# Moving every buffer that TensorE reads to a 512-byte boundary in a two-block sequence-model kernel

## The chip, the cores and the metric

The kernel runs on one core of a Trainium2 chip. The metric is the device time of one launch in microseconds (us); less is better. The program is one straight line of instructions for each engine, tied together by semaphores.

## What is computed

The reference is a small network on 256 tokens of 1024 features, batch 1: two mixer blocks with residuals (a state-space mixer, then latent attention), a norm, and a third block with sparse attention beside a gated convolution, a feed-forward part and a gated embedding. Cut to its shape:

```
h = x
u = rms_norm(h);  h = h + ssd_mixer(u) @ ssm_out_w        # projections 1024 -> 2048+4096+32, 2048 -> 1024
u = rms_norm(h);  h = h + mla_mixer(u) @ mla_out_w        # 1024 -> 384+256+64+2048, 16 heads, 2048 -> 1024
h = rms_norm(h)
h = h + (sparse attention and gated convolution of rmsnorm(h), merged by sigmoid gates) @ w_out_2
h = h + ffn(rmsnorm(h)) @ w_down_2                         # 1024 -> 2 x 2816 -> 1024
h = h + ple_gate(rmsnorm(h)) * (p @ w_ple_2)
out = rmsnorm(h)
```

Nearly all of the arithmetic is in the projections: matrices of weights, in float32, each read once, against 256 tokens.

## The kernel before

**Layout.** Activations lie feature-major: 128 features on the partitions, 256 tokens (1,024 B) along the row. A projection's output tile of 128 features is the sum over its k tiles of `weights[128 x 128].T @ activations[128 x 256]`.

**Precision.** A float32 value is split into a high part in the type float32r and the rest, also float32r. TensorE makes three matmuls for each pair of tiles (lines 628 to 630): weights high by activations high, weights high by activations low, weights low by activations high. In the profile's rows these are `ps<-uh,wh`, `ps<-ul,wh` and `ps<-uh,wl`: what is written, then the moving operand (256 columns of activations, 1,024 B of each partition), then the stationary operand (128 columns of weights, 512 B of each partition). Each matmul has a weight load of its own, a PEld row. In two places the roles are swapped: "V" jobs and "C" jobs (lines 635 to 637, `ps<-wh,uh` and the like) hold activations still and move weights.

**Weights.** They come in 254 slabs of 8 blocks (4,096 B of each partition) through a ring of 6 buffers `raw` (SP issues the loads), ScalarE makes `wh` (line 1122), GpSimd makes `wl` (line 571), both with rings of 6. One slab is 8 blocks, and so 24 matmuls. The order of the jobs is written out by hand in `weight_jobs`, and no scheduler moves anything.

**Memory.** Each `sb(...)` takes the next free bytes of a partition, in the order of the lines, after 16,384 B of DMA scratch and four small constants, so the first one starts at 16,512. Behind them lies an arena of 105 KiB, in which `ar(...)` places the buffers of a phase one behind the other, rounded up to 32 B: `uh`, `ul` (the normed input of every block), then by phase `ynh`, `ynl`, `ogh`, `ogl`, `cqh`, `cql`, `ckh`, `ckl`, `cnh`, `cnl`, `onh`, `onl`, `mh`, `ml`, `cxh`, `cxl`, `ffh`, `ffl`, `ph`, `pl`. A buffer's start is therefore whatever the sizes ahead of it leave. A row of `uh` is 1,024 B and a block of `wh` 512 B, so all rows and blocks of a buffer have the start's remainder by 512.

Of the kernel before, what the change touches and what calls it, by code (L numbers as in the profile page):

```python
# [18 lines left out]
P = 128  # L19
T = 256  # L20
TB = T // P
DM = 1024
KD = DM // P
# [33 lines left out]
FIRST_SLABS = 2  # L57
FIRST_COLS = 8
WARM_UP = 20


def weight_jobs():
# [186 lines left out]
def vector_columns():  # L249

    at, c = {}, 0
    for name, n in [("norm0", 8), ("norm1", 8), ("final1", 8), ("sconv_w", SSM_CT * SSM_TAPS), ("sconv_b", SSM_CT),
                    ("ssm_d", 16), ("ssm_nw", 16), ("dt_bias", 1), ("a_log", 1), ("qnorm", 3), ("kvnorm", 2),
                    ("g_mix", 8), ("pos_k", 16), ("pos_v", 16), ("conv_w", CONV_CT * CONV_TAPS), ("conv_b", 4),
                    ("ln_g", 4), ("ln_b", 4), ("b_co", 8), ("g_ffn", 8), ("fconv_w", 2 * KF * FF_TAPS),
                    ("fconv_b", 2 * KF), ("g_ple", 8), ("g_final", 8)]:
        at[name] = c
        c += n
    return at, c
# [7 lines left out]
def build(nc, slabs_dram, vec_dram, const_dram, x_dram, p_dram, out_dram):  # L267
# [4 lines left out]
    VC, n_vec = vector_columns()  # L272
    ctx = ExitStack()
    with ctx:
        def sb(name, shape, dt=f32):
            return ctx.enter_context(nc.sbuf_tensor(name, shape, dt))


        raw = sb("raw", [P, RAW_RING, SLAB])
        wh = sb("wh", [P, PART_RING, SLAB], f32r)  # L280
        wl = sb("wl", [P, PART_RING, SLAB], f32r)
        h = sb("h", [P, KD, T])
        sq = sb("sq", [P, KD, T])
        vec = sb("vec", [P, n_vec])
        cst = sb("cst", [P, N_CONST])
        ident_b = sb("ident_b", [P, P], bf16)
        mask_s = sb("mask_s", [P, P], bf16)
        cmp_add = sb("cmp_add", [P, P], bf16)
        ones = sb("ones", [P, P])
        sqsum = sb("sqsum", [P, 2, T])  # L290

        msq, root, step = sb("msq", [P, 2 * TB]), sb("root", [P, 2 * TB]), sb("step", [P, 2 * TB])
        late = sb("late", [P, T])
        late_tok = sb("late_tok", [P, TB])
        root1 = sb("root1", [P, TB])
        gain12 = sb("gain12", [P, KD])
        ident = cst[:, 0:128]
        swap = cst[:, 128:256]
        cmp_ok = cst[:, 896:1024]
# [9 lines left out]
        cursor = [0]  # L309
# [3 lines left out]

        def ar(name, shape, dt=f32):
            n = int(np.prod(shape)) * 4
            t = nc.alloc_sbuf_tensor_at(name, [P] + list(shape), dt, offset=base + cursor[0])
            cursor[0] += -(-n // 32) * 32
            assert cursor[0] <= arena_kb * 1024, (name, cursor[0])
            return t


        HEADS = 4
        phase()
        uh, ul = ar("uh", [KD, T], f32r), ar("ul", [KD, T], f32r)
        after_u = cursor[0]
        ynh, ynl = ar("ynh", [16, T], f32r), ar("ynl", [16, T], f32r)
        xs, bT, cT = ar("xs", [16, T]), ar("bT", [8, T]), ar("cT", [8, T])
        acp = ar("acp", [3 * P], f32r)
        sel = ar("sel", [SSM_H], f32r)
# [119 lines left out]
        def sem(name):  # L449
            if name not in sems:  # L450
                sems[name] = ctx.enter_context(nc.semaphore(name))
            return sems[name]
# [140 lines left out]
        def _(pe):  # L593
# [103 lines left out]
            pe.wait_ge(sem("memset"), 2)  # L697
            for _ in range(WARM_UP):
                nc.tensor.matmul(PS_TR[:, 0:P], ones[:], ones[:], start=True, stop=True)
# [1643 lines left out]
```

## Time and profile before

| | |
|---|---|
| median of 3 runs | 867.47 us (866.96 to 868.33) |
| profiled execution, first to last instruction | 865.4 us |
| TensorE (PE) busy, matmul records | 847.8 us, 98% of the span, 7,055 records |
| weight loads (PEld) busy | 816.2 us |
| GpSimd / VectorE / ScalarE busy | 624.1 / 526.8 / 485.7 us |
| DMA queues | 51.9% of 16 engines' span on the weights' queue |
| mean granted TensorE clock | 0.994 of full speed |

How to read it: matmul records overlap, since each one lasts some 280 ns in the trace while the next starts some 118 ns after it. Busy time and the mean duration of a matmul therefore don't tell the engine's pace. Its pace is the distance from one start to the next, which a timeline gives in full and a table by windows gives as length over count (about two matmuls more are counted than start inside a window, because records reach over its edges).

### The profile page before, as it was taken

To read this page: it belongs to the slowest core of one execution; us is meant where nothing else is said; L and a number is where in the kernel's file an instruction comes from. 1 tells how busy PE (TensorE), PEld (TensorE's weight loads), DVE (VectorE), ACT (ScalarE), POOL (GpSimd) and SP (SyncE) were. 2 spreads that over 40 slices of the span, in tenths; PEclk is the share of its full clock that TensorE was granted. 3 is DMA by queue.
4 is the path that set the end of the run, shared out by engine and by line. 5 is a ranking of instruction groups with operands and counts; after the bars stand their busy time and mean duration, and the time that the engine had idled before them with its cause. 6 is when DMAs were issued, how large, how long until landed. Compare 5 with 4: busy or idle time off the path is not lost.

```text
span 865.4 us, 18278 instructions
## 1 busy us (share of the span) xinstructions
PE 847.8 (98%) x7055; PEld 816.2 (94%) x7055; DVE 526.8 (61%) x1543; ACT 485.7 (56%) x925; POOL 624.1 (72%) x282
## 2 busy tenths in 40 slices
PE   8999999999999999999999999999999999999995
PEld 8999988889998899999999999988999999999995
DVE  5997758883243535445458998875566676641164
ACT  6755476664446456563846457875644544554361
POOL 4899756655997455563979899455868888889680
PEclk9999999999999999999999999999999999999997
DMA  8666633332774343433566577433646666667511
GB/s 331 192 219 218 193 99 98 99 98 75 220 218 155 114 145 107 140 99 122 162 204 190 180 210 222 127 95 116 184 144 204 177 192 182 187 193 221 170 49 50
DMA packets 38678, 138.46 MB, mean 160 GB/s; under 512 B 4416, under 2 KB 4544, under 8 KB 38592
## 3 DMA queue, kind: packets, MB, share of 16 engines
q1 hardware_dynamic: 38592, 137.30, 51.9%
q8 instruction: 56, 0.92, 0.5%
q14 instruction: 30, 0.25, 0.1%
HBM read 136.23 MB, written 1.05 MB: 159 GB/s over the span
## 4 chain that ended last, share of the span: by engine, by line
PE 80%; DVE 4%; issue 2%; ACT 1%; POOLq 0%; POOL 0%; ACTq 0%; DVEq 0%
PE ps L628 22%; PE ps L629 22%; PE ps L630 21%; DVE ps L1720 1%; PE ps L850 1%; PE ps L756 1%; PE ps L673 1%; PE ps L655 1%; PE ps L637 1%; PE ps L635 1%; PE ps L636 1%; PE ps L874 1%; PE ps L983 1%; PE ps L846 1%; PE ps L821 1%
## 5 line engine op out<-in xcount | busy, mean ns | idle before, releaser
L571 POOL TENSOR_TENSOR wl<-raw,wh 128x1024 fp32r<-128x1024 f32 x254 | 606.9, 2413 | 199.1 <-ACT wh L1122 198.9
L628 PE MATMUL ps<-uh,wh 128*128 128x256 f32 (+1 forms) x1248 | 352.4, 282 | 1.9 <-POOL wl L571 0.8
L629 PE MATMUL ps<-ul,wh 128*128 128x256 f32 (+1 forms) x1248 | 348.7, 279 | 0.0
L630 PE MATMUL ps<-uh,wl 128*128 128x256 f32 (+1 forms) x1248 | 348.3, 279 | 0.0
L1122 ACT ACTIVATE wh<-raw 128x1024 fp32r<-128x1024 f32 (+1 forms) x255 | 262.9, 1052 | 85.8 <-PE ps L630 77.9
L628 PEld LDWEIGHTS ps<-uh,wh 128*128 128x128 f32 (+1 forms) x1248 | 233.8, 187 | 3.7 <-issue 1.6
L629 PEld LDWEIGHTS ps<-ul,wh 128*128 128x128 f32 (+1 forms) x1248 | 233.7, 187 | 0.0
L630 PEld LDWEIGHTS ps<-uh,wl 128*128 128x128 f32 (+1 forms) x1248 | 233.2, 187 | 0.1
L1813 DVE TENSOR_TENSOR h<-ps,h 128x256 f32<-128x256 f32 x32 | 13.6, 425 | 103.8 <-PE ps L630 103.7
L629 PE MATMUL ps<-ffl,wh 128*128 128x256 f32 x176 | 49.3, 280 | 0.0
L628 PE MATMUL ps<-ffh,wh 128*128 128x256 f32 x176 | 49.1, 279 | 0.0
L630 PE MATMUL ps<-ffh,wl 128*128 128x256 f32 x176 | 49.1, 279 | 0.0
L1720 DVE SCALAR_TENSOR_TENSOR ps<-cpad,vec,ps 128x256 f32<-128x256 f32 x120 | 48.6, 480 | 0.0
L1611 DVE TENSOR_TENSOR fraw<-ps,late 128x256 f32<-128x256 f32 x44 | 18.4, 421 | 38.7 <-PE ps L630 38.6
L1720 DVE SCALAR_TENSOR_TENSOR ps<-sraw,vec,ps 128x256 f32<-128x256 f32 x96 | 38.9, 478 | 0.0
L1720 DVE SCALAR_TENSOR_TENSOR ps<-fraw,vec,ps 128x256 f32<-128x256 f32 x88 | 38.1, 481 | 0.0
L628 PE MATMUL ps<-ynh,wh 128*128 128x256 f32 x128 | 36.1, 282 | 0.0
L628 PE MATMUL ps<-ogh,wh 128*128 128x256 f32 x128 | 36.1, 282 | 0.0
L630 PE MATMUL ps<-ynh,wl 128*128 128x256 f32 x128 | 35.8, 280 | 0.0
L629 PE MATMUL ps<-ynl,wh 128*128 128x256 f32 x128 | 35.7, 279 | 0.0
L630 PE MATMUL ps<-ogh,wl 128*128 128x256 f32 x128 | 35.7, 279 | 0.0
L629 PE MATMUL ps<-ogl,wh 128*128 128x256 f32 x128 | 35.6, 278 | 0.0
(363 smaller groups left out, 1690.8 us busy)
## 6 DMA issues: line engine op xcount, KB each, us to landing
raw<-slabs SPq DMA_DIRECT2D x255, 512.0 KB, 4.0
h<-x_fm SPq DMA_DIRECT2D x4, 256.0 KB, 4.1
out_fm<-outb SPq DMA_DIRECT2D x4, 256.0 KB, 2.2
cst<-shape_consts SPq DMA_DIRECT2D x1, 768.0 KB, 8.4
vec<-vectors SPq DMA_DIRECT2D x1, 299.5 KB, 8.6
pin<-p_fm SPq DMA_DIRECT2D x1, 256.0 KB, 3.8
raw<-slabs SPq DMA_DIRECT2D x1, 128.0 KB, 2.8
vec<-vectors SPq DMA_DIRECT2D x1, 4.0 KB, 2.4
```

The source lines that it names most:

```text
L571: nc.gpsimd.tensor_tensor(wl[:, s % PART_RING, :], raw[:, s % RAW_RING, :], wh[:, s % PART_RING, :].bitcast(f32), ALU.subtract).then_inc(s ...
L628: nc.tensor.matmul(res, w_h, a_h, start=first, stop=False)
L629: nc.tensor.matmul(res, w_h, a_l, start=False, stop=False)
L630: ins = nc.tensor.matmul(res, w_l, a_h, start=False, stop=last)
L635: nc.tensor.matmul(res, a_h, w_h, start=first, stop=False)
L636: nc.tensor.matmul(res, a_h, w_l, start=False, stop=False)
L637: ins = nc.tensor.matmul(res, a_l, w_h, start=False, stop=last)
L655: ins = nc.tensor.matmul(PS_M[:, n.col + c:n.col + c + 1], src[:, b * P:(b + 1) * P], ones[:, 0:1], start=n.summed or k == g * per, stop=n ...
L1122: nc.scalar.activation(wh[:, s % PART_RING, 0:n], raw[:, s % RAW_RING, 0:n], ACT.Copy)\
L1611: tt(dst, o[0:rows, 0:T], late[0:rows, :], ALU.mult).then_inc(sem("dve_evac"), 1)
L1720: return stt(dst, src, w, dst, ALU.mult, ALU.add)
L1813: tt(h[:, k, :], o[:, 0:T], h[:, k, :], ALU.add).then_inc(sem("dve_evac"), 1)
```

## The change

No instruction is added, removed or moved on any engine: the five engines' lists are the same row for row but for the source's line numbers. The memory map changes alone.

- A helper `start_at` puts a gap before the next `sb` buffer, so that it begins at a multiple of 512. It stands ahead of `raw`, `wh`, `wl`, ahead of `h`, and ahead of `ones`.
- `vec` and the small columns (`msq`, `root`, `step`, `late_tok`, `root1`, `gain12`) are allocated first, ahead of the slabs.
- `ar` rounds the start of each buffer of 512 B or more up to a multiple of 512, and of 256 to 511 B up to a multiple of 256.

```diff
+PIECE = 512
+STATIONARY_AT = 0
...
+        def start_at(offset):
+
+            gap = (offset - nc.sbuf_base) % PIECE
+            if gap:
+                sb(f"gap{nc.sbuf_base}", [P, gap // 4])
+
+        vec = sb("vec", [P, n_vec])
+        msq, root, step = sb("msq", [P, 2 * TB]), sb("root", [P, 2 * TB]), sb("step", [P, 2 * TB])
+        late_tok = sb("late_tok", [P, TB])
+        root1 = sb("root1", [P, TB])
+        gain12 = sb("gain12", [P, KD])
+        start_at(STATIONARY_AT)
         raw = sb("raw", [P, RAW_RING, SLAB])
         wh = sb("wh", [P, PART_RING, SLAB], f32r)
         wl = sb("wl", [P, PART_RING, SLAB], f32r)
+        start_at(0)
         h = sb("h", [P, KD, T])
         sq = sb("sq", [P, KD, T])
-        vec = sb("vec", [P, n_vec])
...
+        start_at(0)
         ones = sb("ones", [P, P])
...
         def ar(name, shape, dt=f32):
             n = int(np.prod(shape)) * 4
+            if n >= PIECE // 2:
+                cursor[0] += -cursor[0] % (PIECE if n >= PIECE else PIECE // 2)
             t = nc.alloc_sbuf_tensor_at(name, [P] + list(shape), dt, offset=base + cursor[0])
```

What comes out of it, as the start's remainder by 512 and, in brackets, by 128:

```
buffers                                              before       after
raw, wh, wl, h, sq                                   128 (0)      0
uh, ul, ynh, ynl, ogh, ogl, cqh, cql, ckh, ckl,
ffh, ffl, xs, vn, bT, cT, qr, kr, kn, qn             448 (64)     0
cnh, cnl, gm                                         96 (96)      0
mh, ml, onh, onl, cxh, cxl, ph, pl, npn, npT         480 (96)     0
pn, pT                                               64 (64)      0
ones, sqsum                                          256 (0)      0
cst, ident_b                                         0            0
```

A remainder of 64 by 128 is still a multiple of 64; one of 96 is a multiple of 32 only.

## Rows read from the trace of the kernel before

**Rows 1.** The page, parts 1 and 2: busy TensorE and its granted clock

```profile
PE 847.8 (98%) x7055; PEld 816.2 (94%) x7055; DVE 526.8 (61%) x1543; ACT 485.7 (56%) x925; POOL 624.1 (72%) x282
...
PEclk9999999999999999999999999999999999999997
```

**Rows 2.** Waits of TensorE: total us, times, longest

```profile
PE ps L673 <- DVE root L1572: 2.5, 1, 2.5
PE ps L1089 <- ACT sq L1135: 1.9, 1, 1.9
```

**Rows 3.** Groups of matmuls by form: count, busy us, mean ns

```profile
L628 PE MATMUL ps<-uh,wh 128*128 128x256 f32 x1240 | 350.0, 282 | 1.9 <-POOL wl L571 0.8 <-DVE wl L1657 0.5 <-DVE gm L1611 0.3
...
L629 PE MATMUL ps<-ffl,wh 128*128 128x256 f32 x176 | 49.3, 280 | 0.0
...
L628 PE MATMUL ps<-ynh,wh 128*128 128x256 f32 x128 | 36.1, 282 | 0.0
L628 PE MATMUL ps<-ogh,wh 128*128 128x256 f32 x128 | 36.1, 282 | 0.0
...
L628 PE MATMUL ps<-cqh,wh 128*128 128x256 f32 x72 | 21.2, 295 | 0.0
...
L628 PE MATMUL ps<-mh,wh 128*128 128x256 f32 x64 | 18.1, 282 | 0.0
...
L628 PE MATMUL ps<-onh,wh 128*128 128x256 f32 x32 | 9.2, 288 | 0.0
...
L628 PE MATMUL ps<-ph,wh 128*128 128x256 f32 x16 | 4.6, 289 | 0.0
```

**Rows 4.** Windows: us, busy (and count) of PE, PEld, DVE, ACT, POOL; clock, DMA

```profile
645.00:820.00 175.00, 175.00 (x1488) 175.00 (x1487) 91.56 (x239) 85.29 (x121) 148.07 (x62) 1.00 0.64 189
...
604.00:636.00 32.00, 32.00 (x269) 32.00 (x269) 17.92 (x49) 19.38 (x34) 26.31 (x11) 1.00 0.59 186
```

**Rows 5.** Windows over eight stretches with a denser rhythm, and their sum

```profile
141.60:144.10 2.50, 2.50 (x23) 2.50 (x24) 2.25 (x10) 1.57 (x4) 1.13 (x1) 1.00 0.70 188
...
399.50:415.60 16.10, 16.10 (x140) 15.99 (x140) 9.55 (x18) 6.24 (x14) 5.02 (x4) 1.00 0.24 67
...
sum 46.10, PE 46.10 PEld 45.99 DVE 32.33 ACT 25.96 POOL 30.35; mean PE 5.76 PEld 5.75 DVE 4.04 ACT 3.24 POOL 3.79
```

**Rows 6.** Timeline of TensorE, 402 to 416.5 us: start us, duration, instruction

```profile
402.12 0.28 PE L628 MATMUL ps<-ogh,wh 128*128 128x256 f32 x1
...
415.49 0.28 PE L629 MATMUL ps<-ogl,wh 128*128 128x256 f32 x1
415.60 0.28 PE L630 MATMUL ps<-ogh,wl 128*128 128x256 f32 x1
415.72 0.32 PE L628 MATMUL ps<-ogh,wh 128*128 128x256 f32 x1
415.87 0.28 PE L629 MATMUL ps<-ogl,wh 128*128 128x256 f32 x1
```

**Rows 7.** Timeline where the roles are swapped: weights move, activations stand

```profile
489.11 0.28 PE L635 MATMUL ps<-wh,uh 128*128 128x256 f32 x1
...
494.10 0.28 PE L637 MATMUL ps<-wh,ul 128*128 128x256 f32 x1
...
500.12 0.29 PE L637 MATMUL ps<-wh,cxl 128*128 128x256 f32 x1
...
501.90 0.28 PE L637 MATMUL ps<-wh,cxl 128*128 128x256 f32 x1
```

**Rows 8.** Timeline of the float32r matmuls that move 64 columns

```profile
525.15 0.28 PE L629 MATMUL ps<-hgl,wh 128*128 128x64 f32 x1
...
526.26 0.28 PE L630 MATMUL ps<-hgh,wl 128*128 128x64 f32 x1
```

**Rows 9.** The page, part 5: what GpSimd and ScalarE do for each slab

```profile
L571 POOL TENSOR_TENSOR wl<-raw,wh 128x1024 fp32r<-128x1024 f32 x254 | 606.9, 2413 | 199.1 <-ACT wh L1122 198.9
...
L1122 ACT ACTIVATE wh<-raw 128x1024 fp32r<-128x1024 f32 (+1 forms) x255 | 262.9, 1052 | 85.8 <-PE ps L630 77.9
```

More of the change, by code:

```diff
@@ L288, in build @@
         cmp_add = sb("cmp_add", [P, P], bf16)
+        start_at(0)
         ones = sb("ones", [P, P])
         sqsum = sb("sqsum", [P, 2, T])
-        msq, root, step = sb("msq", [P, 2 * TB]), sb("root", [P, 2 * TB]), sb("step", [P, 2 * TB])
         late = sb("late", [P, T])
-        late_tok = sb("late_tok", [P, TB])
-        root1 = sb("root1", [P, TB])
-        gain12 = sb("gain12", [P, KD])
         ident = cst[:, 0:128]
```

## The prediction

> **What bounds the kernel now.** I read the page first: TensorE is busy 98% of the span, and its clock is granted in full in all slices but the last [rows 1]. The waits agree: the longest of TensorE's own is 2.5 us, the next 1.9 us [rows 2]. So the time is TensorE's pace, and nothing else is worth reading until that pace is known. The groups by form give the counts, three matmuls for each row shown [rows 3]. Those with a moving operand at remainder 448 are `uh` 1,240, `ff` 176, `yn` 128, `og` 128, `cq` 72 and a group `ck` of 32: 3 x 1,776 = 5,328 matmuls. Those with an operand that is a multiple of 32 only are `mh` 64, `on` 32, `ph` 16, and `cn` and `cx`, 32 each: 3 x 176 = 528. With 48 `wh,uh` that makes 5,904, all 256 columns wide. The mean durations there, 279 to 295 ns, say nothing of the pace.
>
> The pace is in the windows. From 645 to 820 us, the feed-forward part, 1,488 records lie in 175 us, two of them from over the edge: 175 / 1,486 = 117.8 ns from start to start [rows 4]. From 604 to 636 us, where `mh` and `ml` and `onh` move, it is 32 / 267 = 119.9 ns [rows 4]. 256 columns at the granted level of 2.4 GHz are 106.7 ns, so 11 ns of each matmul are not columns. At 117.8 ns the 5,904 matmuls are 695 us of 865: one nanosecond of pace is worth 5.9 us.
>
> **Does the pace depend on addresses?** Three readings.
>
> First, the same buffers run at two paces. From 402.12 to 415.49 us there are 118 steps on `ogh`, `ogl` (remainder 448): 13.37 / 118 = 113.3 ns [rows 6]. Then one matmul comes late (415.72 to 415.87, 150 ns instead of 113), and the same buffers go on at 117.8 ns. There are eight such dense stretches, 46.1 us in all [rows 5], about 400 matmuls. The DMA share is 0.70 in one of them and 0.24 in another, 0.64 in the stretch at 117.8 ns [rows 4, 5], so it isn't traffic. It reads like a rhythm between the two reads that TensorE makes at once, the moving rows and the next weights: a rhythm that a disturbance can set to either of two modes, and which then stays.
>
> Second, the swapped jobs. With the weights moving (remainder 128, a multiple of 128) and `uh` standing (448), the last 44 steps of the job take 4.99 us, 113.4 ns [rows 7]. With `cxh`, `cxl` standing (480, a multiple of 32 only) 15 steps take 1.78 us, 118.7 ns [rows 7]. Same line, same shape, same moving buffer: only the stationary address differs.
>
> Third, the multiples of 32: 119.9 against 117.8 ns, as above. So operands that are off a 64-byte boundary cost 2 to 5 ns, and a moving operand on a multiple of 128 was always in the dense mode in the one job that has both on multiples of 64.
>
> **The parts of the change.** (a) 5,328 matmuls: moving operand from 448 to 0, weights from 128 to 0. (b) 528 matmuls: from a multiple of 32 to 0. (c) the 48 swapped ones: 128 and 448 to 0 and 0. (d) `vec` and the small columns move ahead of the slabs, `ones`, `sqsum`, `pn` and the like are realigned: no instruction is added, so the cost is nothing unless an access gets slower; VectorE and ScalarE have 39% and 44% of the span free [rows 1]. If that cover were gone, a whole slab's work would show: GpSimd takes 2.41 us and ScalarE 1.05 us for each slab [rows 9], and TensorE takes 24 x 117.8 = 2.83 us.
>
> The trace has no matmul with both operands on 0, so the new pace is bounded by rows. Below: the 64-column float32r matmuls make 10 steps in 1.11 us, 111 ns, though they have a quarter of the columns [rows 8]; that is what a weight load of its own leaves, and a step can't be much shorter. Above: 119.9 ns, the worst steady pace seen [rows 4]. I take 113.3 ns, the dense mode, because the change puts the moving operand where it stood in rows 7 and because it is a mode that these very buffers already reach.
>
> The sum, against the profiled execution (865.4 us):
> - (a) about 350 of the 5,328 are in the dense mode already, and some 80 have a wait in their step. 4,900 x (117.8 - 113.3) = 22.0 us.
> - (b) some 500 without a wait, 500 x (119.9 - 113.3) = 3.3 us.
> - (c) and (d): nothing.
> - Given back: TensorE waits little now, and would wait for GpSimd only below 2.41 / 24 = 100.5 ns a step, so nothing is taken off. A slab would take 2.72 us.
>
> Together 25.3 us, so 840.1 us in the profile. The profiled span is 2.1 us under the median of the runs, and 867.5 - 25.3 = 842.2; **I forecast 842 us**.
>
> **A page that says otherwise.** The Trainium skill, page "TensorE: Matmul & The Clock Gate", section "Step-by-step: what each phase is for", says that TensorE has two independent read ports into SBUF and that loading the next tile's weights takes no bandwidth from the running matmul; its section "Back-to-back issue gap" gives columns / 2.4 + 2.5 ns, an estimate of 109.2 ns here. By that every matmul here would run at 109.2 ns before and after, and the change would do nothing. The trace differs, 117.8, 113.3 and 119.9 ns at one shape, so I keep the rows. The rule that addresses don't matter is the second rival below, worked out from rows there.
>
> **The rivals.**
>
> *More than the dense mode (0.22).* If the extra time is an access more because a row straddles a boundary, the aligned read loses it altogether and the weight load is left, 111 ns [rows 8]. Then (a) is 4,900 x 6.8 = 33.3 us, the 350 dense ones give 350 x 2.3 = 0.8, and (b) 500 x 8.9 = 4.5: 38.6 us, so 829 us. For it: off-boundary operands cost time already. Against it: in no place does a 256-column matmul go below 113.
>
> *The addresses don't decide the mode (0.22).* The two modes stand at the same addresses in rows 6, so alignment to 64 may be all that addresses do, and the mode is set by chance. Then (a) stays at 117.8, and (b) falls to it: 500 x 2.1 = 1.1 us, 866.4 us, 0.13% and no change that can be measured. For it: `ogh` in both modes. Against it: the swapped job, dense in 44 steps on end. If not even the multiples of 32 gain, it is 867.5 us. This is the case that the skill's page on TensorE stands for.
>
> *The two reads meet (0.18), the case on the other side.* Now the moving rows and the weights start at different remainders (448 and 128, or 128 and 448). Afterwards both start at 0. If the two reads collide when they want the same slice of the memory at once, equal starts are the worst case, and every matmul takes at least the pace of the worst stretch: 5,328 x 2.1 = 11.2 us, the 350 dense ones lose 350 x 4.5 = 1.6 more, (c) 0.3: +13 us, 880.5 us. It decides from a mean of 118.1 ns on, 0.3 ns x 5,904 = 1.8 us or 0.2%. For it: the two modes look like two phases of just such a meeting. Against it: they have met in some way in all stretches, since a sweep over 1,024 B beside one over 512 B passes every remainder, and 118 is what that gives.
>
> **How the numbers follow.** The forecast has 0.38. A change of under 0.2%, 1.7 us, can't be told from none in a measurement of this kernel. Faster is the forecast and the first rival, with a mixture of modes that gives part of the 25 us counted to the forecast: 0.38 + 0.22 = 0.60. Same is 0.21, since a sliver of the second rival would fall above 0.2%; slower is 0.19. The range goes from 827 us, just below the 111 ns case, to 872 us, past the no-change case and into the small end of the collision: it leaves out most of the 0.18 of that rival. The likeliest case's own range is 836 to 852 us: 836 if the pace is 112.3 ns, 852 if only 60% of (a) goes into the dense mode.
>
> **What would show it.** In the changed kernel's trace the window over the feed-forward part should hold 175 us / 113.3 ns = 1,545 starts for each 175 us instead of 1,486, and `mh`, `ml` the same pace as `uh`, `ul`, with no stretch at 117.8. The waits of TensorE should stay under some 3 us each, and GpSimd's idle time should shrink by about as much as the span. If the windows still show 1,486, the second rival holds; if `mh` alone moves, it holds exactly. If the pace is above 118.1 ns everywhere, the starts at an equal remainder are to blame. My forecast would also be wrong if the pace falls but GpSimd or a DMA becomes what TensorE waits for, which the waits would name.

## The result and the profile after

The changed kernel takes 878.98 us (median of 4 runs, 878.83 to 879.70), the kernel before 867.82 us on the same chip (866.96 to 868.33). The ratio is 1.013, with a 95% interval of 1.0116 to 1.0145: **the change made the kernel slower by 11.2 us**, where 25 us of gain were forecast. That is under 2%, but far outside what the runs of either kernel differ by. The profiled execution spans 877.2 us, 11.8 us more than that of before.

The page's line of busy time and its line of TensorE's clock answer to [rows 1], its two group lines to [rows 9]:

```profile
PE 860.2 (98%) x7055; PEld 829.0 (95%) x7055; DVE 529.8 (60%) x1543; ACT 485.7 (55%) x925; POOL 623.4 (71%) x282
...
PEclk9999999999999999999999999999999999999998
...
L583 POOL TENSOR_TENSOR wl<-raw,wh 128x1024 fp32r<-128x1024 f32 x254 | 606.1, 2412 | 211.4 <-ACT wh L1134 211.1
...
L1134 ACT ACTIVATE wh<-raw 128x1024 fp32r<-128x1024 f32 (+1 forms) x255 | 262.7, 1051 | 89.3 <-PE ps L642 85.5
```

The picture is the same one, stretched: TensorE busy for 98% at a full clock, the other engines with the same work, and more idle time before GpSimd's slabs (211.4 us instead of 199.1), because the ring comes free later. ScalarE's and GpSimd's groups have the same durations. VectorE is busy for 3.0 us more (529.8 instead of 526.8), in a few single operations; the largest change is one addition to `h` near the end, the longest of eight in this row, 2.68 us where the longest before was 1.85. No wait of TensorE grew by it:

```profile
L2233 DVE TENSOR_TENSOR h<-h,pt x8: 424/504/2682, 842.9 to 865.4; 128x256 f32<-128x256 f32 x8
```

TensorE's waits answer to [rows 2] and haven't moved:

```profile
PE ps L685 <- DVE root L1584: 2.5, 1, 2.5
PE ps L1101 <- ACT sq L1147: 1.9, 1, 1.9
```

So again only the pace is left. The first window of [rows 4], then a window inside the same `ogh`, `ogl` matmuls that were dense in [rows 6]; they stand later in the trace than before, since the kernel is slower. Columns as there. Under it are the same two matmuls of the swapped job as in [rows 7]:

```profile
645.00:820.00 175.00, 175.00 (x1462) 175.00 (x1461) 95.95 (x261) 84.93 (x120) 145.78 (x62) 1.00 0.60 184
...
408.00:420.00 12.00, 12.00 (x102) 12.00 (x101) 7.21 (x12) 4.13 (x10) 1.53 (x1) 1.00 0.13 42
```

```profile
495.94 0.28 PE L647 MATMUL ps<-wh,uh 128*128 128x256 f32 x1
...
501.22 0.28 PE L649 MATMUL ps<-wh,ul 128*128 128x256 f32 x1
```

175 us over 1,460 matmuls are 119.9 ns a step, where before it was 117.8. The dense `ogh`, `ogl` stretch of [rows 6] has gone as well: 12 us over 100 matmuls are 120.0 ns, where it was 113.3. So has that of the swapped job: 44 steps in 5.28 us are 120.0 ns, where it was 113.4. There is nearly one pace now and no other. Counted start by start over the whole trace, leaving out each step over 126 ns (those hold a wait):

```
float32r matmuls of 256 columns     before     after
steps                                5,789     5,790
mean                              117.6 ns  119.9 ns
sum                               680.9 us  694.2 us
at 115 ns or less                      425        13
at 119 to 121 ns                       703     5,514
```

The sums differ by 13.3 us, and nothing else in TensorE's trace grew. Taken from start to start, waits included, these got shorter: the table's own matmuls with steps over 126 ns by 0.6 us, the float32 ones without a split by 0.35 us (119.0 to 118.7), the 48 with 512 columns by 0.3 us (without waits from 233.3 to 227.8 ns each), and the small float32r ones by 0.2 us. 13.3 - 1.45 = 11.85 us, the 11.8 us of the span.

### The profile page after: what moved, and what is told of

It is laid out like the page before. It is cut to its first block, busy times and chain, and to the rows that moved or that the text cites. A ratio compares the mean times of both kernels' runs of the same rounds, so it can differ in the third digit from the quotient of the medians.

```text
span 877.2 us, 18278 instructions
## 1 busy us (share of the span) xinstructions
PE 860.2 (98%) x7055; PEld 829.0 (95%) x7055; DVE 529.8 (60%) x1543; ACT 485.7 (55%) x925; POOL 623.4 (71%) x282
## 4 chain that ended last, share of the span: by engine, by line
PE 80%; DVE 4%; issue 2%; ACT 1%; POOLq 0%; POOL 0%; ACTq 0%; DVEq 0%
PE ps L640 22%; PE ps L641 22%; PE ps L642 22%; DVE ps L1732 1%; PE ps L862 1%; PE ps L768 1%; PE ps L685 1%; PE ps L647 1%; PE ps L649 1%; PE ps L648 1%; PE ps L667 1%; PE ps L886 1%; PE ps L995 1%; PE ps L858 1%; PE ps L833 1%
## 5 line engine op out<-in xcount | busy, mean ns | idle before, releaser
L583 POOL TENSOR_TENSOR wl<-raw,wh 128x1024 fp32r<-128x1024 f32 x254 | 606.1, 2412 | 211.4 <-ACT wh L1134 211.1
L640 PE MATMUL ps<-uh,wh 128*128 128x256 f32 (+1 forms) x1248 | 357.0, 286 | 1.8 <-POOL wl L583 0.7
L642 PE MATMUL ps<-uh,wl 128*128 128x256 f32 (+1 forms) x1248 | 353.0, 283 | 0.0
L641 PE MATMUL ps<-ul,wh 128*128 128x256 f32 (+1 forms) x1248 | 353.0, 283 | 0.0
L640 PEld LDWEIGHTS ps<-uh,wh 128*128 128x128 f32 (+1 forms) x1248 | 238.6, 191 | 3.4 <-issue 1.6
L641 PEld LDWEIGHTS ps<-ul,wh 128*128 128x128 f32 (+1 forms) x1248 | 238.7, 191 | 0.1
L642 PEld LDWEIGHTS ps<-uh,wl 128*128 128x128 f32 (+1 forms) x1248 | 238.6, 191 | 0.1
```

Of the source, the lines that this page charges most:

```text
L583: nc.gpsimd.tensor_tensor(wl[:, s % PART_RING, :], raw[:, s % RAW_RING, :], wh[:, s % PART_RING, :].bitcast(f32), ALU.subtract).then_inc(s ...
L640: nc.tensor.matmul(res, w_h, a_h, start=first, stop=False)
L641: nc.tensor.matmul(res, w_h, a_l, start=False, stop=False)
L642: ins = nc.tensor.matmul(res, w_l, a_h, start=False, stop=last)
```

## The experiments

The question is what about an address sets the pace. In the expectations, **Theory A** is that the absolute place of an operand decides, and **Theory D** that the difference between the starts of the moving and the stationary operand does. **Theory E** is about a second thing, the choice between the two modes at one address: the way in which the run of matmuls was entered decides. "By 256" means that only a start's remainder by 256 bytes counts. Paces in the tables are (start of the last matmul - start of the 9th) / 15 for each series of 24.

### A map of the pace: m1_map

A kernel of its own, which computes nothing of the network: 256 series of 24 float32r matmuls in the pattern of lines 628 to 630, on buffers filled from `x`, with the start of the moving rows and of the weights stepped through 0 to 448 by 64 bytes, and four ways to enter a series: entry 0 straight after the series before, entries 1 to 3 after one matmul of 128 columns, of 1 column and of 64 columns. This kernel and the five of its kind below ran once each.

```diff
+for k in range(ROWS):
+    a, b = m // 4 + k * T, s // 4 + k * P
+    hi, lo = mvh[:, a:a + WIDE], mvl[:, a:a + WIDE]
+    w_h, w_l = wh[:, b:b + P], wl[:, b:b + P]
...
+    nc.tensor.matmul(res, w_h, hi, start=k == 0, stop=False)
+    nc.tensor.matmul(res, w_h, lo, start=False, stop=False)
+    ins = nc.tensor.matmul(res, w_l, hi, start=False, stop=k == ROWS - 1)
```

> A kernel of its own: nothing of the network is computed. 256 series of 24 matmuls, each in the three-matmul pattern of the projections (float32r, 256 columns moving, 128 columns standing), with the start of the moving rows and of the stationary blocks set to each pair of remainders 0, 64, ... 448 by 512, and each pair four times: straight behind the series before, or behind one float32 matmul of 128 columns, one of 1 column, or one float32r matmul of 64 columns. Theory D (the two reads meet, so only the difference of their remainders counts): one value along each diagonal of equal difference; 120.0 ns where the difference (moving minus stationary) is 0, 117.8 or 113.3 where it is 320, 113.3 where it is 192. Theory A (an absolute boundary counts, of the moving rows alone): 120.0 ns in the whole row of moving remainder 0, whatever the stationary remainder, and 117.8 or 113.3 at 448. Theory E (the entry sets the mode): the pace differs between the four entries of one pair more than between pairs.

The timeline of TensorE in two of its series, entered alike, both with the moving rows at 0; first the weights at 256, then at 320, which are 0 and 64 by 256:

```profile
220.29 0.28 PE L102 MATMUL ps<-mvh,wh 128*128 128x256 f32 x1
...
221.73 0.28 PE L102 MATMUL ps<-mvh,wh 128*128 128x256 f32 x1
...
223.28 0.28 PE L104 MATMUL ps<-mvh,wl 128*128 128x256 f32 x1
...
224.64 0.28 PE L104 MATMUL ps<-mvh,wl 128*128 128x256 f32 x1
```

Each pair of rows is 12 steps apart: 1.44 us, 120.0 ns, and 1.36 us, 113.3 ns. The pairs of the first two entries, in ns a step; rows and columns from 256 to 448 repeat those from 0 to 192 nearly everywhere:

```
                     weights at   0      64     128    192
entry 0, moving at   0          120.0  117.8  118.7  117.8
                    64          117.8  120.0  113.3  118.7
                   128          118.7  117.8  120.0  117.8
                   192          117.7  118.7  117.8  120.0
entry 1, moving at   0          120.0  113.3  118.7  117.8
                    64          117.7  119.9  113.3  118.7
                   128          118.7  117.8  120.0  117.8
                   192          113.3  118.7  117.8  120.0
```

Equal starts give 119.6 to 120.0 ns wherever they lie, and with each entry: Theory A falls. D holds, by 256 bytes and not by 512. With d = (moving - stationary) by 256, and 64 series for each d over all four entries: d = 0 gives 120.0; d = 128 gives 118.7 in 58 and 120 in 6; d = 64 gives 117.8 in 60 and 113.3 in 4; d = 192 gives 113.3 in 38 and 117.8 in 26. So the difference settles which paces are possible. What picks between two isn't settled by the entry alone (E): moving at 0 and weights at 64, in entry 1, ran at 113.3 ns here and at 117.8 ns in m2_map32 and m3_map16. This puts the kernels in their places: before, 448 - 128 = 320, d = 64; after, d = 0; the swapped job of [rows 7], 128 - 448, d = 192.

### Only the weights' start: s320, s192, s128, and both moved: both128

Four kernels with everything aligned as in the changed one, and only the starts of the two groups of buffers chosen, so that D and A part. What stands behind `#` is added here and isn't in the code.

```diff
-STATIONARY_AT = 0
+STATIONARY_AT = 320        # s320: d = 192.  s192: 192, d = 64.  s128: 128, d = 128
...
+        start_at(128)       # both128 alone, with STATIONARY_AT = 128: d = 0
         arena = sb("arena", [P, arena_kb * 256])
```

> The changed kernel with the weight slabs at remainder 320 instead of 0, so that moving minus stationary is 192 by 512, as in the swapped job of the kernel before (113.3 ns). Theory D: pace 113.3 ns in all projections, 5,790 x 6.7 ns = 38 us less than the changed kernel, about 841 us. Theory A (moving rows at 0 are slow by themselves): 120.0 ns and 879 us again.

> The changed kernel with the weight slabs at remainder 192, so that moving minus stationary is 320 by 512, as in the kernel before. Theory D: 117.8 ns with stretches of 113.3, so the time of the kernel before, 866 to 868 us, though every moving row starts at a multiple of 512. Theory A: 120.0 ns and 879 us.

> The changed kernel with both the weight slabs and the arena of the activations at remainder 128: no operand starts at a multiple of 512 any more, but the two remainders are equal. Theory D: 120.0 ns and 879 us, as the changed kernel. Theory A: as the kernel before or better, 842 to 868 us.

> The changed kernel with the slabs at remainder 128: difference 128 by 256, all activations at 0. By the first map (118.7 ns in most entries at moving 0, stationary 128) the pace falls by 1.3 ns from 120.0: 5,790 x 1.3 = 7.5 us under the changed kernel, 871.5 us. If the number of operands on a 512 B boundary counted instead, half of the way back to the kernel before or all of it: 867 to 873, with 117.8 ns in the windows.

```
            d     time (median)             ratio to before        mean step
s320       192    855.28 (852.24 to 858.44)  0.986 (0.983 to 0.989)  116.1 ns
s192        64    866.15 (865.13 to 867.36)  0.998 (0.997 to 0.999)  117.3 ns
s128       128    872.67 (872.25 to 873.23)  1.005 (1.004 to 1.007)  118.7 ns
both128      0    879.18 (878.88 to 880.60)  1.014 (1.012 to 1.015)  119.9 ns
```

The feed-forward window in the four traces, in the order of this table:

```profile
645.00:820.00 175.00, 175.00 (x1489) 175.00 (x1488) 91.34 (x249) 85.08 (x120) 144.63 (x62) 1.00 0.62 185
```

```profile
645.00:820.00 175.00, 175.00 (x1488) 175.00 (x1487) 90.90 (x237) 84.45 (x120) 148.00 (x62) 1.00 0.63 189
```

```profile
645.00:820.00 175.00, 175.00 (x1478) 175.00 (x1477) 93.38 (x244) 84.51 (x119) 146.66 (x63) 1.00 0.62 189
```

```profile
645.00:820.00 175.00, 175.00 (x1462) 175.00 (x1461) 95.75 (x261) 84.92 (x120) 145.86 (x62) 1.00 0.61 183
```

The count in brackets behind PE is the pace: 1,489 and 1,488 are 117.7 and 117.8 ns, 1,478 is 118.6, 1,462 is 119.9. both128, with none of these operands at 0, is the changed kernel over again, with the same counts for TensorE. s192 keeps the activations at 0, and is back at the time of before within 0.2%. So the whole loss is d = 0. s128 came out as the map's 118.7 ns says (871.5 us expected), and not at the 117.8 ns of the theory that counts operands on a boundary. The 1.5 us by which s192 is under before have a place too: `mh`, `ml`, `onh` and `onl`, at d = 96 before, are at d = 64 there, and their 285 steps fell from 120.0 to 113.4 ns, 1.9 us.

s320 gains 12 us, but not the 26 expected with every step at 113.3: 2,289 of its 5,786 steps are dense (115 ns or less) and the long feed-forward stretch isn't. Its timeline has the late matmul of [rows 6]:

```profile
410.66 0.28 PE L641 MATMUL ps<-ogl,wh 128*128 128x256 f32 x1
410.77 0.28 PE L642 MATMUL ps<-ogh,wl 128*128 128x256 f32 x1
410.89 0.32 PE L640 MATMUL ps<-ogh,wh 128*128 128x256 f32 x1
411.04 0.28 PE L641 MATMUL ps<-ogl,wh 128*128 128x256 f32 x1
...
411.40 0.28 PE L641 MATMUL ps<-ogl,wh 128*128 128x256 f32 x1
...
437.47 0.34 PE L640 MATMUL ps<-uh,wh 128*128 128x256 f32 x1
```

One matmul lasts 0.32 us, and the next comes 158 ns after it instead of 113. It is the same matmul of the program as at 415.72 us before. But here the dense mode is back four steps on: from 411.40 to 437.47 us there are 230 steps, 113.3 ns each. Before, the same event was followed by 117.8 ns. The step behind this matmul is long (143 to 158 ns) in all seven kernels whose `og` matmuls were dense there (before, s192, s320, m64s128, two_gaps, and the two wl448 kernels below), and isn't in the changed kernel, both128 and s128. In before and s192, both at d = 64, 117.8 ns followed; in s320, m64s128, two_gaps and wl448 the dense mode was back within four steps.

### Does alignment play any part: m64s128, two_gaps

m64s128 has d = 192 with other absolute places (activations at 64, weights at 128). two_gaps is the kernel before with none of the change in it and two unused columns of 128 bytes: `vec` stays behind `sq`, `mh` and `onh` stay on multiples of 32 only, and nearly all other pairs get d = 192 (activations at 192, weights at 256).

```diff
--- before.py
+        sb("gap0", [P, 32])
         raw = sb("raw", [P, RAW_RING, SLAB])
...
+        sb("gap1", [P, 32])
         arena = sb("arena", [P, arena_kb * 256])
```

> The changed kernel with the arena of the activations at remainder 64 and the slabs at 128: difference 192 by 256, as in the kernel with the slabs at 320, but at the pair that the map shows dense in three of four entries. Theory D alone: the same time as that kernel, 855 us, with the same mixture of 113.3 and 117.8. If the start by itself matters for which of the two modes is taken (the map: at moving 0, straight behind another series, 117.8; at 64, 113.3), more of the matmuls are dense: 842 to 852 us.

> The kernel before with nothing of the change: only 128 B left free ahead of the weight slabs and 128 B ahead of the arena. The slabs then start at 256 and the activations at 192 (by 512), difference 192 by 256, the multiples of 32 stay off a boundary, and vec and the small columns stay where they were. Theory D: as the changed kernel with its slabs at 320, 853 to 860 us, a mixture of 113.3 and 117.8 ns. A theory in which the 512 B starts of the change itself give the gain of that kernel, or the place of vec does: 867 us.

m64s128 took 860.45 us (852.71 to 861.29), ratio 0.990 (0.986 to 0.993); two_gaps 861.01 us (858.68 to 861.91), ratio 0.993 (0.991 to 0.994). Their dense steps are 1,840 of 5,788 and 1,927 of 5,775. m64s128 missed both of its expected values (855 us, or 842 to 852), and two_gaps is 1 us over the top of its 853 to 860. Two gaps in the kernel before are worth 6.4 us; full alignment with the same d = 192 is worth 7.1 us at m64s128's starts and 12.4 us at s320's. So the boundaries and the place of `vec` aren't needed for the gain, and m64s128 shows no clear gain from them. Whether they have a part in s320's further 5 to 6 us isn't settled. These kernels vary from run to run by more than before does (m64s128 by 8.6 us, s320 by 6.2, before by under 2), and the profiled runs of the three lie within 2.4 us. How many steps find the dense mode, none of the theories forecast.

### What is it in the difference: m2_map32, m3_map16, m4_wide512, m5_next, m6_bf16

Kernels of their own again, on m1's pattern, and again without the network's computation.

```diff
-COMBOS = [(m, s, e) for e in range(4) for m in range(0, 512, 64) for s in range(0, 512, 64)]
+# m2: both by 256 in steps of 32.  m3: moving by 64, stationary in steps of 16
+# m4: WIDE = 512.  m5: the low rows and low weights shifted apart from the high ones, in steps of 32
+# m6: bf16 operands at the same byte addresses
```

> The map of the first kernel of its own again (nothing of the network is computed), now by 256 and in steps of 32 B for both operands, each pair with the four entries. Theory D, as the first map leaves it: the value depends on the difference by 256 and is the worst, 120.0 ns, at difference 0 and also at 32 off the others in some pairs, since the kernel before had 119.9 at 480 against 128 (difference 96 by 256) and 118.7 at 128 against 480 (160). A theory of separate boundaries (a row off a multiple of 64 costs by itself) expects all eight rows and columns at odd multiples of 32 to be slow, whatever the difference.

> The same in steps of 16 B for the stationary operand alone, the moving one at 0, 64, 128 and 192. If the memory is read in slices of 64 B, a stationary start off such a boundary should look like a mixture of its two neighbours, 117 to 120 ns, and never be denser than 113.3. If slices are smaller, a denser value than at any multiple of 64 may show.

> The same with 512 moving columns for each matmul, starts by 256 in steps of 64 B. 512 columns at 2.4 GHz are 213.3 ns; the V jobs of the kernel before took 233.5 ns at moving 128, stationary 448 (difference 192 by 256). Theory D: the value depends on the difference here too, about 20 ns above the columns' time, by a few ns more at difference 0. If only the phase at the end of a short matmul mattered, it would be the same for all pairs.

> A kernel of its own, nothing of the network is computed. High moving rows at 0 and high weights at 64 (difference 192 by 256); the low moving rows at dm and the low weights at 64 + dw, each pair of dm and dw by 256 in steps of 32 B, with the four entries. Theory N: what meets is the running matmul's moving read and the load of the next matmul's weights. Then the pairs that count are high rows against high weights (fixed) and low rows against low weights (dm - dw), and the map is constant along diagonals of equal dm - dw. Theory O: a matmul's moving read meets its own weights. Then low rows against high weights (dm) and high rows against low weights (dw) count, and the map is a sum of a part of the row and a part of the column, with no diagonals. A pair with a single dense mode, 113.3 ns in all four entries, may show.

> The map once more, nothing of the network computed, with bfloat16 operands in place of float32r: 256 columns of 2 B moving, 128 of 2 B standing, starts by 256 in steps of 64 B, four entries. If what meets is reads of 8 B a cycle and 4 B a cycle, half the bytes leave room: one value for all pairs, near the 107 ns of the columns. If any two reads meet whatever their width, differences between the pairs remain, with the worst at difference 0.

**m2.** With the moving rows at 0, entry 1, and the weights at 0, 32, ..., 224: 120.0, 118.4, 117.8, 117.3, 118.7, 119.8, 117.8, 116.6 ns. Pairs with one or both operands on a multiple of 32 only are not slow by themselves: moving at 32 with weights at 224 ran at 113.3 ns in two entries. Their pace goes with the difference too: a difference of 96 gave 119.7 to 120.3 ns in all its 32 series, one of 224 gave 118.0 to 118.5.

**m3.** With the weights off the multiples of 64, in steps of 16 bytes, the paces at the differences not tried before lie between 116.6 and 120.6 ns, and one pair (192, 240) stood at 123.8 in two of four entries. Sorted by difference they fall together as in m2 (48: 116.6 to 116.8 in all 16 series; 144: 120.0 to 120.6). None is under 113.3 ns: finer placing of the weights' start buys nothing.

**m4.** With 512 columns a step, entry 0, in ns (the other entries within 1.3); a miss, since d = 0 was expected to be the worst and is the best:

```
                weights at   0      64     128    192
moving at   0              226.7  233.5  232.4  228.9
           64              228.9  226.7  233.5  232.4
          128              232.3  228.9  226.7  233.5
          192              233.3  232.4  228.9  226.7
```

Again the difference decides, with the two ends exchanged: d = 0 is the best and d = 192 the worst. It is what the wide jobs of the changed kernel did, 233.3 to 227.8 ns.

**m5.** Theories N and O each named which of the reads of neighbouring matmuls meet. Neither fits: the worst entry for each pair follows neither the diagonals nor the sums of a row's and a column's effect. One pair alone is at 113.3 ns in all four entries: low rows in step with the high rows, low weights 128 bytes off the high ones by 256. What meets what stays open, but this gives a placing to try.

**m6.** With bf16 the difference doesn't matter: all pairs run at 109.1 to 109.2 ns. Two rows of its timeline:

```profile
99.90 0.27 PE L102 MATMUL ps<-mvh,wh 128*128 128x256 bf16 x1
...
100.56 0.27 PE L102 MATMUL ps<-mvh,wh 128*128 128x256 bf16 x1
```

Six steps in 0.66 us. So the 4 to 11 ns above that belong to operands of 4 bytes, not to 256 columns as such; whether to the moving or to the stationary one, m6 doesn't part. The estimate of 109.2 ns from the Trainium skill (page "TensorE: Matmul & The Clock Gate", section "Back-to-back issue gap") is met within 0.1 ns by bf16; for float32r no run came under 113.3. That section gives its formula for an isolated matmul and sets a stream with weight loads apart from it, which the prediction didn't say.

### The placing that stays dense: wl448, wl448_psum

wl448 is s320 with `wl` moved 128 bytes by 256 away from `wh`, the pair that m5 found.

```diff
         wh = sb("wh", [P, PART_RING, SLAB], f32r)
+        start_at(448)
         wl = sb("wl", [P, PART_RING, SLAB], f32r)
```

> The changed kernel with raw and the high weights at remainder 320 and the low weights at 448: by 256, high rows minus high weights 192, and the low weights 128 beyond the high ones. The map of high and low operands shows 113.3 ns for this pair in all four entries, alone among 64 pairs. If the map holds in the kernel, the slow mode is gone: 5,790 matmuls at 113.3 to 113.6 ns, 36 to 38 us under the changed kernel, 841 to 844 us, and the time hardly varies between runs. If the entries of the map are too few and the slow mode can be entered in the kernel, a mixture again: 850 to 860 us.

It took 854.69 us (850.66 to 856.14), ratio 0.984 (0.981 to 0.986), and not the 841 to 844 expected: no faster than s320, and yet 5,092 of its 5,756 steps are dense, with a mean of 114.0 ns. Its feed-forward window:

```profile
645.00:820.00 175.00, 174.73 (x1540) 174.49 (x1539) 94.74 (x258) 88.51 (x126) 151.22 (x65) 1.00 0.64 192
```

The pace is there (175 / 1,538 = 113.8 ns), so something else is lost. TensorE's waits name it, and the window around it shows the clock:

```profile
PE ps L641 <- DVE sraw L1624: 5.1, 1, 5.1
```

```profile
90.00:100.00 10.00, 7.20 (x41) 7.20 (x42) 8.11 (x17) 2.42 (x4) 2.36 (x2) 0.66 0.41 125
```

VectorE's timeline, and under it GpSimd's, show what is late:

```profile
81.53 1.66 DVE L1733 SCALAR_TENSOR_TENSOR ps<-sraw,vec,ps 128x256 f32<-128x256 f32 x4
83.21 9.08 DVE L1761 TENSOR_TENSOR acp<-acr,acp 32x384 fp32r<-32x384 f32 x1
92.32 0.42 DVE L1624 TENSOR_TENSOR sraw<-ps,late 128x256 f32<-128x256 f32 x1
```

```profile
75.39 16.50 POOL L584 TENSOR_TENSOR wl<-raw,wh 128x1024 fp32r<-128x1024 f32 x7
```

A subtraction of 32 x 384 lasts 9.08 us, and 0.55 us in the kernel before:

```profile
L1748 DVE TENSOR_TENSOR acp<-acr,acp x1: 548/548/548, 85.4 to 85.4; 32x384 fp32r<-32x384 f32 x1
```

It has two inputs in SBUF, and it ends when GpSimd's unbroken run of slabs does (the last seven of it in this view, 75.39 + 16.50 = 91.9, beside 92.3 us). In the kernel before, GpSimd had pauses of some 0.4 us between slabs there. Behind the subtraction stands the next `sraw`, and behind that TensorE, which is idle for 5.1 us and then makes 23 steps in 4.91 us, 213 ns each, the level of 1.2 GHz, until its clock is granted in full again:

```profile
93.18 0.42 PE L642 MATMUL ps<-ul,wh 128*128 128x256 f32 x1
93.40 0.41 PE L643 MATMUL ps<-uh,wl 128*128 128x256 f32 x1
...
98.09 0.31 PE L641 MATMUL ps<-uh,wh 128*128 128x256 f32 x1
```

In wl448_psum VectorE first copies one of the two inputs to PSUM.

```diff
+                    link(nc.vector.tensor_copy(PS_TR[H, P:4 * P], acr[H, :]))
-                    tt(acp[SSM_H:2 * SSM_H, :], acr[H, :], acp[H, :].bitcast(f32), ALU.subtract)\
+                    tt(acp[SSM_H:2 * SSM_H, :], PS_TR[H, P:4 * P], acp[H, :].bitcast(f32), ALU.subtract)\
                         .then_inc(sem("decay_parts"), 1)
```

> The kernel with high weights at 320 and low weights at 448, and one edit on VectorE: the subtraction that makes the low part of acp no longer reads two operands from SBUF, but one from a PSUM bank, into which a copy of 32 x 384 is made first. If the 9.08 us of that one operation is a lock-out by GpSimd's back-to-back operations on two SBUF reads, it falls to some 0.5 us each for the copy and the subtraction, TensorE's 5.1 us wait and the half clock behind it (about 12 us together) are gone, and the time is 841 to 844 us. If VectorE is held up there for another reason, the copy takes the 9 us instead and the time stays at 854.

**847.88 us** (847.43 to 849.84), ratio to before 0.978 (0.977 to 0.979): 31 us under the changed kernel and 20 us under the one before, the best here. The copy and the subtraction, then GpSimd's timeline, then the place where TensorE had stood idle and the feed-forward part:

```profile
83.08 0.54 DVE L1761 COPY ps<-acr 32x384 f32<-32x384 f32 x1
83.66 0.55 DVE L1762 TENSOR_TENSOR acp<-ps,acp 32x384 fp32r<-32x384 f32 x1
```

```profile
65.92 30.83 POOL L584 TENSOR_TENSOR wl<-raw,wh 128x1024 fp32r<-128x1024 f32 x13
```

```profile
90.00:100.00 10.00, 10.00 (x91) 10.00 (x90) 7.76 (x20) 5.36 (x9) 9.35 (x5) 1.00 0.72 221
...
645.00:820.00 175.00, 174.73 (x1539) 174.49 (x1539) 93.60 (x250) 90.78 (x129) 151.52 (x64) 1.00 0.62 187
```

The 9.08 us became 0.54 + 0.55, though GpSimd ran without a pause all around them (65.92 to 96.75 us), as in wl448. The clock holds, and TensorE's longest wait is the old 2.5 us. 847.9 us is 4 to 7 us above the 841 to 844 expected; the mean step of 114.0 ns instead of 113.3 explains 5,782 x 0.7 ns = 4 us of it. The wait and the half clock were costed at about 12 us together; they were 5.1 us and 23 x (213 - 113) = 2.3 us, beside 7.8 us between the two profiled spans (853.6 and 845.8).

## Why the prediction was wrong

**What bounds the kernel: right.** TensorE's pace was the whole question, 5.9 us for each ns: 2.3 ns more a step came out as 13 us more in the steps. No wait of TensorE, no other engine and no transfer took part.

**The step that failed is the choice of 113.3 ns for (a)**, "because the change puts the moving operand where it stood in rows 7 and because it is a mode that these very buffers already reach". In rows 7 it was not the moving operand's place that made the job dense. It stood at 128 with the stationary operand at 448, d = 192; the map has 113.3 at just this pair (128, 192) in one entry. The change brings the multiple of 128, as it had there, and not the difference. m1_map and both128 show it: equal starts have the pace of 120.0 ns at each of the eight places tried. Rows 7 already spoke against the reason given: with the same moving buffer at the same place, the `cx` steps ran at 118.7 ns. Term (a), forecast at -22.0 us, measured +12.6 us.

**Second reading, the same buffers in two modes: half right.** The two modes are real and stand at one pair of addresses, and in before a late matmul changed the mode (rows 6). They aren't set by chance alone: the matmuls of `ff` had the slow mode in all 528 steps counted in each of before, s192, s320, m64s128 and two_gaps. And they belong to the differences 64 and 192; d = 0 doesn't have them. "A mode that these very buffers already reach" said nothing about the place they were moved to.

**Third reading and (b): the comparison was right, its reason wrong.** `mh` and `onh` did run at 119.9 ns. I gave it to being off a 64-byte boundary; they had a difference of 480 - 128 = 352, 96 by 256, and m2 shows 119.7 to 120.2 ns for their own pair by 256 (moving 224, weights 128), and 113.3 for other pairs off such a boundary. These stayed, 119.9 to 120.0. The sum of (b) took all of its 528 matmuls at 119.9, though `cx` (118.7 in rows 7) and `cn` were below that: (b), forecast at -3.3 us, measured +0.3.

**(c)** was costed at nothing. The swapped jobs went from 113.4 to 120 ns, 48 x 6.6 = 0.3 us, as the third rival had it. **(d)** was right in what it costs: ScalarE's durations haven't moved, and the few longer operations of VectorE (3.0 us in all) held up nothing. The 48 matmuls of 512 columns weren't costed at all; they gained 0.3 us.

**The rivals.** "The two reads meet" gave what happened, in place, sign and size: 880.5 us worked out, 878.98 measured, past its deciding point of 118.1 ns nearly everywhere. That equal starts are the worst case is shown; that two reads collide is its explanation, and no run shows the reads themselves. With 512 columns equal starts are the best case, which a plain collision doesn't give. What I held against it was that "a sweep over 1,024 B beside one over 512 B passes every remainder, and 118 is what that gives". m1_map refutes that: both sweeps pass all remainders in all pairs, and the phase at which they start still sets the pace. Rows for weighing this were at hand: rows 4 and 7 together hold four pairs of starts, and sorted by their difference they are four differences as well as four places. I sorted them by place only. "More than the dense mode" has no run for it, since no steady pace of float32r matmuls of 256 columns went below 113.3 ns. "The addresses don't decide the mode" falls too: their difference decides which modes there are.

**The page of the Trainium skill** ("TensorE: Matmul & The Clock Gate", "Step-by-step: what each phase is for"), by which loading weights takes nothing from the running matmul's read, fits the bf16 series, which don't depend on the starts, and not the float32r ones, which do (113.3 to 120.0 ns at 256 columns).

**Still open.** Which reads meet, and why 512 columns want d = 0; why one placing has only the dense mode in the map, and nearly only that in the kernel; what picks the mode where there are two; and what makes one and the same matmul of the program late in the seven kernels that are dense there.

## What to carry to other kernels

These rules come from one kernel and its maps; measure before relying on them. When a kernel is bound by TensorE at full clock, divide a long window by its count of matmuls and compare that with the columns; if float32r matmuls with a weight load each stand at 117 to 120 ns, try the starts of moving and stationary buffers in 64-byte steps against each other, and don't give both the same start by 256 bytes: with 256 columns it was the slowest of the 64-byte placings here, with 512 columns the fastest. Rounding everything up to one boundary looks tidy and makes all differences zero. An observation about one operand's address is an observation about a pair: list both before choosing an explanation, and after every speed-up look at the waits again, since a denser TensorE let GpSimd run without a gap and block VectorE.

## What the runs showed of the hardware

- A float32r matmul of 256 columns behind another one takes 113.3, 117.8, 118.7 or 120.0 ns from start to start at starts on multiples of 64, by the difference of its operands' starts by 256 bytes, with equal starts the slowest; 512 columns take 226.7 to 233.6 ns, with equal starts the fastest; bf16 with 256 columns takes 109.1 to 109.2 ns at all differences.
- At one pair of addresses there are two steady modes, 113.3 and 117.8 ns (`ogh`, `ogl` in rows 6). The feed-forward window of 175 us stood at 117.7 to 117.8 ns in all five kernels with d = 64 or 192 for both the high and the low parts.
- A VectorE operation with two inputs in SBUF was held for 9.08 us while GpSimd ran slabs of 2.4 us back to back, over more than one of them. The Trainium skill, page "SBUF — State Buffer", section "🔬 SBUF: two separate sides", says that such an operation and a GpSimd one exclude each other for the whole of an instruction; the trace fits that and goes further, since the end of one instruction (some 2.4 us) did not let this operation in. Elsewhere it did: in the changed kernel an `h<-h,pt`, two inputs in SBUF too, was through after 2.68 us while GpSimd went on without a pause. That it is this lock is argued from the cure, one input moved to PSUM under the same unbroken run of GpSimd, and was not measured apart.
- After 5.1 us idle TensorE made 23 steps of 213 ns, the level of 1.2 GHz, before it was back at the full clock; the window of 10 us had a granted clock of 0.66 (wl448).
